# Expert weight slots that hold half the k-steps of gate and of up, filled by two 1 MB transfers

## The reference

```
xn = rmsnorm(x, g)
grp  = argmax(xn @ w_router_group)            # 4 groups
top2 = top_k(expert logits of that group, 2)  # 8 experts each, 32 in all
for e in range(32):
    h = silu(xn @ w_gate[e]) * (xn @ w_up[e])         # (1024 -> 512), float32
    y = y + combine[:, e:e+1] * (h @ w_down[e])       # (512 -> 1024)
out = rmsnorm(x + y, g_final)
```

## Time and profile before

| | |
|---|---|
| median of 3 runs | 918.31 us (918.26 to 919.07) |
| profiled execution | 917.77 us, span 916.2 us |
| mean granted TensorE clock | 0.943 |
| PE / PEld busy | 803.4 us (88%) / 456.1 us (50%) |
| DVE / ACT / POOL busy | 263.7 / 120.0 / 128.0 us |
| HBM read / written | 245.33 MB / 13.46 MB |
| chain that ended last | PE 61%, DMA 34%, DVE 2%, issue 1% |

### The profile page before, as it was taken

How to read it: one execution, slowest core, us unless ns; L and a number is a source line. 1 busy time by engine, 2 the same in 40 slices (tenths; PEclk the granted TensorE clock), 3 DMA queues, 4 the chain that set the end, 5 groups by cost and what they waited for, 6 DMA issues and landing times.

```text
span 916.2 us, 9588 instructions
## 1 busy us (share of the span) xinstructions
PE 803.4 (88%) x3838; PEld 456.1 (50%) x3839; DVE 263.7 (29%) x745; ACT 120.0 (13%) x230; POOL 128.0 (14%) x224
## 2 busy tenths in 40 slices
PE   2999999999999899959997797779778887888786
PEld 2788888778888655533333233233223332333332
DVE  3799756410011245451110111011101110111115
ACT  3210030120000223400000000000000000000012
POOL 3000005860033200010110101010101000100000
PEclk9999999999999999959998898899989898989898
DMA  9420121335200393149999999999999999999926
GB/s 313 128 93 24 69 104 37 109 129 180 92 1 0 140 425 130 47 157 428 424 429 426 428 426 426 426 427 426 427 427 426 426 426 429 426 427 428 378 69 253
DMA packets 41663, 251.58 MB, mean 275 GB/s; under 512 B 13061, under 2 KB 13913, under 8 KB 28786
## 3 DMA queue, kind: packets, MB, share of 16 engines
q1 hardware_dynamic: 34284, 236.97, 63.0%
q0 software_dynamic: 6672, 12.86, 3.9%
q10 hardware_dynamic: 662, 1.13, 0.4%
HBM read 245.33 MB, written 13.46 MB: 282 GB/s over the span
## 4 chain that ended last, share of the span: by engine, by line
PE 61%; DMA 34%; DVE 2%; issue 1%; ACTq 0%; ACT 0%; SPq 0%; DVEq 0%; POOLq 0%
DMA arena<-in_w_exp_up 32%; PE ps L1369 26%; PE ps L1619 12%; PE ps L1515 6%; PE ps L1632 5%; PE ps L1691 2%; PE ps L1454 1%; PE ps L1449 1%; PE ps L1611 1%; PE ps L1503 1%; PE ps L1537 1%; DVE arena L829 1%; DMA arena<-in_cache_pool 1%; ACTq L588 0%; DVE arena L782 0%
## 5 line engine op out<-in xcount | busy, mean ns | idle before, releaser
L1619 PE MATMUL ps<-arena 128*64 128x512 f32 x1024 | 256.7, 659 | 70.0 <-DMA arena<-in_w_exp_up 68.9
L1369 PE MATMUL ps<-arena 128*128 128x272 f32 x1024 | 238.8, 395 | 0.0
L1369 PEld LDWEIGHTS ps<-arena 128*128 128x128 f32 x1024 | 195.5, 191 | 39.8
L1619 PEld LDWEIGHTS ps<-arena 128*64 128x64 f32 x1024 | 86.9, 152 | 217.2 <-issue 215.1
L1632 PE MATMUL ps<-arena 128*64 128x512 f32 x512 | 116.4, 595 | 1.3 <-DVE arena L1280 1.3
L1284 DVE TENSOR_SCALAR arena<-ps,arena 128x512 f32<-128x512 f32 x32 | 24.0, 751 | 214.1 <-PE ps L1632 214.1
L782 DVE TENSOR_TENSOR arena<-arena 128x256 f32<-128x256 f32 (+10 forms) x223 | 75.5, 339 | 11.4 <-ACT arena L689 3.9
L1252 DVE TENSOR_TENSOR arena<-ps,arena 128x1024 f32<-128x1024 f32 x16 | 19.6, 1224 | 190.1 <-PE ps L1611 190.1
L1632 PEld LDWEIGHTS ps<-arena 128*64 128x64 f32 x512 | 37.9, 137 | 64.8 <-issue 61.4
L546 POOL DMA_INDIRECT y_parts<-arena x32 | 31.9, 997 | 267.8 <-DVE arena L1284 267.8
L732 ACT ACTIVATE arena<-ps,arena 128x512 f32<-128x512 f32 x32 | 22.0, 687 | 324.5 <-PE ps L1619 324.5
(11 more groups left out here) (222 smaller groups left out, 484.4 us busy)
## 6 DMA issues: line engine op xcount, KB each, us to landing
arena<-in_w_exp_gate SPq DMA_DIRECT2D x32, 2048.0 KB, 27.9
arena<-in_w_exp_up SPq DMA_DIRECT2D x32, 2048.0 KB, 32.3
arena<-in_w_exp_down SPq DMA_DIRECT2D x32, 2048.0 KB, 37.4
arena<-in_w_in SPq DMA_DIRECT2D x6, 2048.0 KB, 8.9
arena<-in_x_prompt SPq DMA_DIRECT2D x8, 512.0 KB, 6.6
arena<-in_w_out SPq DMA_DIRECT2D x2, 2048.0 KB, 10.2
arena<-y_parts SPq DMA_DIRECT2D x4, 1024.0 KB, 8.3
arena<-in_w_glu_a SPq DMA_DIRECT2D x1, 2048.0 KB, 10.5
```

Source lines behind the costliest of these rows:

```text
L1369: last = pe.matmul(dst[:, hh, 0:HALF], w[:, k, m * P:(m + 1) * P], rhs[:, k, hh * HALF:(hh + 1) * HALF], start=(k == 0), stop=(k == kk - 1))
L1619: last = pe.matmul(ps[n * TILE:(n + 1) * TILE, 2 + par, :], x_t[:, k, :], w[:, k, :], start=(k == 0), stop=(k == KD - 1))
```

## The change

Load l of an expert now brings part l % 3. Part 0 is the first four k-steps of gate (first half of the slot) and of up (second half), part 1 is the last four of both, and part 2 is down as before. Every part is brought by two transfers of 1 MB with 8 KB a partition, so that a slot's semaphore counts 32 for a filling instead of 16; down too comes in two. `gate_up` is called twice for an expert, each time over four k-steps behind a wait for one slot, and accumulates in the same PSUM banks; the first call gives back its slot by a new semaphore `gu_half`, the second by `gu_done`. The overflow path (rows beyond 64 for an expert) calls `gate_up` as before, with whole matrices.

```
-            l = 3 * e + kind
-            return ring[l % NS].rearrange("p (k n) -> p k n", k=4 if kind == 2 else KD), w_arr[l % NS], 16 * (l // NS + 1)
+            l = 3 * e + part
+            return ring[l % NS].rearrange("p (k n) -> p k n", k=4 if part == 2 else KD), w_arr[l % NS], 32 * (l // NS + 1)
...
+            half_slot = SLOT // 2
             def load(l):
-                sp.dma_start(ring[l % NS], experts[l % 3][l // 3]).then_inc(w_arr[l % NS], 16)
+                e, part = divmod(l, 3)
+                for n in range(2):
+                    kind, first = (2, n) if part == 2 else (n, part)
+                    sp.dma_start(ring[l % NS][:, n * half_slot:(n + 1) * half_slot],
+                                 experts[kind][e][:, first * half_slot:(first + 1) * half_slot]).then_inc(w_arr[l % NS], 16)
...
-                e, kind = divmod(l - NS, 3)
-                if kind == 2:
-                    sp.wait_ge(down_done, e + 1)
-                else:
-                    sp.wait_ge(gu_done, e + 1)
+                e, part = divmod(l - NS, 3)
+                sp.wait_ge((gu_half, gu_done, down_done)[part], e + 1)
                 load(l)
...
-            def gate_up(par, x_t, w_gate, w_up):
-                for k in range(KD):
+            def gate_up(par, x_t, w_gate, w_up, first=0, steps=KD, done=gu_done):
+                for k in range(steps):
                     for n, w in enumerate((w_gate, w_up)):
-                        last = pe.matmul(ps[n * TILE:(n + 1) * TILE, 2 + par, :], x_t[:, k, :], w[:, k, :],
-                                         start=(k == 0), stop=(k == KD - 1))
-                last.then_inc(gu_done, 1)
+                        last = pe.matmul(ps[n * TILE:(n + 1) * TILE, 2 + par, :], x_t[:, first + k, :], w[:, k, :],
+                                         start=(first + k == 0), stop=(first + k == KD - 1))
+                last.then_inc(done, 1)
...
-                    gate_up(e % 2, xg_t[e // 2 % 2][:, :, e % 2 * TILE:(e % 2 + 1) * TILE], weights(e, 0), weights(e, 1))
+                    x_t = xg_t[e // 2 % 2][:, :, e % 2 * TILE:(e % 2 + 1) * TILE]
+                    for part in range(2):
+                        w = weights(e, part)
+                        gate_up(e % 2, x_t, w[:, 0:4], w[:, 4:8], 4 * part, 4, (gu_half, gu_done)[part])
```

More of the change, by code:

```diff
@@ L293, in encoder_step @@
         xt_done, xt_ready = sem("xg_turned"), sem("xg_t_ready")
+        gu_half = sem("gate_up_half_done")
         gu_done, gu_copied, gu_turned = sem("gate_up_done"), sem("gate_up_copied"), sem("gate_up_turned")
@@ L310, in w_slot, with expert_w @@
             return slot(s).rearrange("p (k n) -> p k n", k=k)
-        def expert_w(e, kind):
-            l = 3 * e + kind
-            return ring[l % NS].rearrange("p (k n) -> p k n", k=4 if kind == 2 else KD), w_arr[l % NS], 16 * (l // NS + 1)
+        def expert_w(e, part):
+            l = 3 * e + part
+            return ring[l % NS].rearrange("p (k n) -> p k n", k=4 if part == 2 else KD), w_arr[l % NS], 32 * (l // NS + 1)
         def overflow(eng, body, first=None):
@@ L1634, in down, with weights @@
                 last.then_inc(down_done, 1)
-            def weights(e, kind):
-                view, arrived_at, count = expert_w(e, kind)
+            def weights(e, part):
+                view, arrived_at, count = expert_w(e, part)
                 pe.wait_ge(arrived_at, count)
```

## The result

| | before | changed |
|---|---|---|
| median of 20 runs each | 919.41 us (915.83 to 922.15) | 921.86 us (918.66 to 923.93) |
| ratio of the runs | 1 | 1.0021 (95% interval 1.0011 to 1.0031) |
| profiled execution, span | 917.77 us, 916.2 us | 923.93 us, 922.3 us |
| mean granted clock | 0.943 | 0.966 |

By this ratio the change costs 1.9 us (1.0 to 2.9); the two medians differ by 2.45. That is at the 1.84 us that I had named as the limit of what can be told, but 20 runs of each tell it from none. The first profile of the changed kernel is 6.1 us longer than that of before, so more than half of that difference belongs to these two executions and not to the change.

The account below looks back on a forecast made before the run. The byte stream up to the last up weights, and the work behind that landing, bound the kernel. Stream +6.2 and +0.4, less 5.86 in the tail, gave +0.7 us: 919.0 us, 8 in 10 within 915.3 to 922.6.

Parts of the forecast that it names:

- The tail: Behind the last landing, half of expert 31's gate/up product remains instead of all: 5.86 us saved.
- The clock part: In expert 31's gate/up product, 2.3 of the 5.86 us saved come from full instead of low granted clock.
- the term for an overrun: Expert 31's first half at low clock running past the last landing: taken as 0, bound 2.2 us.
- The packets: Each weight load as two 8 KB-a-partition transfers costs 0.07 us more, over 88 loads +6.2 us; bounds 0 and +9.7.
- dear packets: In the weight stream, 8 KB packets cost 315 ns, 0.11 us a load: +4.2 us, 921.5 to 924.7; 31 in 100.
- The scatter: One more GpSimd scatter of product rows goes ahead of the last gate/up landing: +0.4 us, bounds 0 and 0.4.
- SyncE: Twice as many loads issued, 0.43 us each, six in a row 2.6 us, covered by a 30 us backlog.
- The sum: End of expert 31's gate/up product moves by +0.7 us, all behind it unchanged; median 919.0 us.
- the likeliest case: Whole kernel: no difference that can be told, 919.0 us, own range 917.0 to 920.1; 51 in 100.
- Cheap packets: In the weight stream, the boundary between two transfers costs nothing: -5.5 us, 912.8 us; 15 in 100.
- transfers that do not overlap: In the weight stream, each transfer begins only after the previous one landed: 240 us more, 1159 us; 1 in 100.
- halves that land together: Expert 31's halves share the engines and land with the second load; product ends 6.6 us later, 924.9 us; 2 in 100.

Follow-up runs that it names:

- filler kernel: Kernel before plus 15 identity matmuls ahead of TensorE's wait for expert 31's gate and up; 917.23 us beside 919.66, ratio 0.9979.

## Why the prediction held

1. *The tail.* Predicted 9.41 - 3.55 = 5.86 us saved. Measured 9.41 and 8.70 before, 3.65 after: 5.8 and 5.1, mean 5.4. The clock part is the one that varies from profile to profile: the same whole product behind the same kind of wait took 9.74, 9.46 and 8.47 us in the three kernels with smaller packets. The first half ran at the low level for part of it in two profiles of three (granted clock 0.72 and 0.74, and 1.00 in the third), and the time between the landings (4.9 us forecast, 5.4 in the first profile) took that up: the term for an overrun, put at 0, was right; the idle time ahead of it was 2.69, forecast 2.6.

2. *The packets.* Predicted 88 x 0.07 = 6.2 us. The kernel that has nothing but this gives +6.5 over the first profile of before, and 6.3 over 462.8, the mean of three streams with whole loads (462.6, 463.4, and 462.3 of the filler kernel). Of my two readings of the earlier trace rows the landings were the better one, but that their 0.07 is so near the 0.073 measured is in part luck, since the tenths in those rows allowed 0 to 0.14. By the packet shares the changed kernel has 4637 us / 14736 = 315 ns a packet, just what the dear rival named, and still the loss is not 0.11. The bytes show where the rest went: 122.51 MB in 300 us are 5.14 us a load, 120.72 MB are 5.21, so +0.08, while the share of queue 1 rose from 96.0 to 96.6%. Of the longer packets 0.03 us a load fell into time in which the engines had no packet of this queue before; the reading by packet shares left that out.

3. *The scatter*, predicted +0.4. The changed kernel's stream is on average 469.8, +7.0 over 462.8, so some 0.7 more than with two transfers alone, and the landings of expert 31's halves are 5.4 us apart in the first profile, where two 1 MB transfers alone take 5.0 at 421 GB/s. It fits, but was not tried by itself.

4. *SyncE*, predicted 0.43 us an issue and hidden. Hidden it is, but the size was wrong by far; see below.

5. *The sum*: predicted +0.7; by the profiles 7.0 - 5.4 = +1.6 us; measured +1.9 (1.0 to 2.9). The part behind the product, which I had taken as unchanged, was 1.1 us longer in the mean of the few profiles; with it they would give +2.7, so that 1.6 lies so near 1.9 proves little. Mechanism, place and sign were right, both large terms to within 0.5 us; but being the small difference of two large terms, the sum moved by more than half of the line that I had drawn, and lies on it. The measured 921.86 us are 2.9 above the 919.0 forecast, outside the likeliest case's own range (917.0 to 920.1) and at the time that I had given to dear packets. 1.1 of the 2.9 are the kernel before, whose median rose from 918.31 in 3 runs to 919.41 in 20. That the forecast of no difference that can be told came out is thus narrow, and in part luck. Of the 0.9 us that are missing up to 1.6, the stream has 0.4 more than forecast, and the tail gave 0.5 less, because the low clock covered less of the last product in the second profile of before. The step that was sized worst for the sum is thus the clock part of the tail: I took its 2.3 us from one execution as if each had it. Of the rivals, dear packets asked for 0.11 us a load and decided from 0.083 on; two transfers alone cost 0.073, and the changed kernel's 7.0 / 88 = 0.080 comes close to that line. By its own sum that rival's time was 918.3 + 4.2 = 922.5 us, not the 921.8 that stands there, and no sum gives the 921.5 at which its range begins. Cheap packets fell by the stream of 469, transfers that do not overlap by the two and four transfers, and halves that land together by the rows of 869.45 and 874.74. The 2 us that the prediction took from the Trainium skill (DMA: Bandwidth & Descriptors, section Anatomy of one DMA) for a DMA are given there for the path that GpSimd issues on, and these loads are SyncE's; with four transfers a load instead of two, none of it shows in the time. The Trainium skill's packet overhead (DMA: Bandwidth & Descriptors, section Why small descriptors are slow), an estimate of 3.5 ns a packet from its cycles, is short of the 9 to 10 ns that three kernels show here; the measurement decides.

## What to carry to other kernels

In a stage that the DMA engines bound, as here, a finer step pays only behind the last landing, and its price is paid on every load: apply it to the last expert's gate and up alone (-4.3 us here) rather than to all (+1.9 us). Keep the longest contiguous run per partition in the bulk (here 16 KB, which gave 427 GB/s, beside 421 with 8 KB and 409 with 4 KB). When one wait at the end is gone, add up what TensorE still has to do from there before moving more work: here it was at once the bound.

## What was not expected of the hardware

SyncE's issues, 0.33 to 0.43 us in the kernel before, mostly take 2.1 us and more in the later stage of the changed kernel. SyncE in order of time:

```profile
842.10 2.12 SPq L395 DMA_DIRECT2D arena<-in_w_exp_up  x1
844.26 2.11 SPq L395 DMA_DIRECT2D arena<-in_w_exp_gate  x1
846.41 2.13 SPq L395 DMA_DIRECT2D arena<-in_w_exp_up  x1
...
852.52 5.62 SPq L416 DMA_DIRECT2D arena<-x_rows  x1
858.19 8.63 SPq L419 DMA_DIRECT2D arena<-x_rows  x1
```

The stream moves one such transfer of 1 MB in 15.43 / 6 = 2.6 us, so this looks like an issue that waits for room; no run tries it. The time from issue to landing shrinks: 28.3 us for the last up half, 34.5 for the whole up load before, and with 4 KB packets less again, here with two and then with four transfers a load:

```profile
867.27 19.20 DMA arena<-in_w_exp_up
```

```profile
872.67 15.85 DMA arena<-in_w_exp_up
```

What is in flight is thus nearer to a fixed number of packets than of bytes, at an estimate some 28.3 / 0.315 = 90 of 8 KB, 19.2 / 0.16 = 120 or 15.85 / 0.16 = 100 of 4 KB an engine, 0.7 against 0.5 and 0.4 MB; what sets the limit is not shown. It cost nothing here since the stream never ran dry (share 1.01) and what stands behind on SyncE, the loads of x2_rows, had time: they landed by 884.9, and TensorE's additions began at 889.66. In a kernel whose SyncE also issues something urgent it could cost time.
